# Where the last quarter of an output projection stands: between the values of the seventh and the eighth head

## What is computed

```python
z = rmsnorm(h) @ w_in                        # q latent, kv latent, rope key, and q, f, i, g of the recurrence
q = rmsnorm(cq) @ w_uq ; ckv = rmsnorm(...)  # 8 heads of 64 + 32, chunk-causal mask
o_mla = softmax(q k^T) v                     # attention over meta tokens and the blocks so far
S = diag(f_t) S + (1 - f_t) i_t^T            # gated recurrence, 4 heads of 128 x 128
o_hg = rmsnorm(S^T q_t) * silu(g)
h = h + concat(o_mla, o_hg) @ w_o            # output projection, 1024 x 1024
h = h + moe(rmsnorm(h))                      # top-1 group of 4, top-2 of its 4 experts, 16 experts of width 256
y = rmsnorm(h)
```

## Time and profile before

| what | us |
|---|---|
| median of 3 runs | 1286.23 (1285.06 to 1296.19) |
| the profiled execution's own time | 1288.34 |
| its span, first to last instruction | 1286.4 |
| input phase | 0 to 263.5 |
| preparation | 263.5 to 310.8 |
| passes 0 to 7 | 310.8 to 773.9 |
| pass 8 and the last projection | 773.9 to 850.7 |
| barrier and routing | 850.7 to 882.4 |
| experts | 882.4 to 1253.9 |
| combination and output | 1253.9 to 1286.4 |

### The profile page before, as it was taken

How to read it: one execution, slowest core, us unless ns; L and a number is a source line. 1 busy time by engine, 2 the same in 40 slices (tenths; PEclk the granted TensorE clock), 3 DMA queues, 4 the chain that set the end, 5 groups by cost and what they waited for, 6 DMA issues and landing times.

```text
span 1286.4 us, 18334 instructions
## 1 busy us (share of the span) xinstructions
PE 1104.2 (86%) x5855; PEld 888.5 (69%) x5855; DVE 734.0 (57%) x1348; ACT 519.3 (40%) x935; POOL 376.3 (29%) x378
## 2 busy tenths in 40 slices
PE   5999999969878989899899999945889899898940
PEld 4898899945466777777777786734667777677730
DVE  4320510146656656656465654447776778777866
ACT  4434122123422222322323222305777778777713
POOL 2100400001621111101010101103565666666657
PEclk9999999978989899999999998976999999999985
DMA  7340141141787666574545453805987676776567
GB/s 268 95 152 1 58 136 48 48 105 43 261 268 279 220 214 216 209 247 162 197 148 197 148 181 139 294 33 196 328 284 258 225 260 229 252 237 213 221 220 262
DMA packets 105765, 242.84 MB, mean 189 GB/s; under 512 B 15248, under 2 KB 63840, under 8 KB 95456
## 3 DMA queue, kind: packets, MB, share of 16 engines
q0 software_dynamic: 23328, 122.17, 27.1%
q1 hardware_dynamic: 81600, 117.94, 27.0%
q10 hardware_dynamic: 768, 1.84, 0.4%
HBM read 243.31 MB, written 48.94 MB: 227 GB/s over the span
## 4 chain that ended last, share of the span: by engine, by line
PE 56%; DMA 11%; DVE 10%; issue 9%; ACT 6%; POOL 4%; SPq 2%; POOLq 1%; ACTq 0%; DVEq 0%
DMA below<-in_w 8%; PE ps L1007 6%; PE ps L879 4%; PE ps L897 4%; PE ps L2103 4%; PE ps L2105 4%; PE ps L2104 4%; PE ps L966 3%; DVE low L1761 3%; PE ps L1045 3%; PE ps L1046 3%; PE ps L1049 3%; PE ps L2098 3%; PE ps L2097 3%; PE ps L2099 2%
## 5 line engine op out<-in xcount | busy, mean ns | idle before, releaser
L1761 DVE TENSOR_TENSOR low<-below,high 128x1024 fp32r<-128x1024 f32 x128 | 192.1, 1547 | 72.9 <-ACT high L1459 59.7
L1429 POOL TENSOR_TENSOR low<-below,high 128x1024 fp32r<-128x1024 f32 x64 | 146.5, 2307 | 105.9 <-ACT high L1480 105.9
L1557 PE MATMUL ps<-high 128*128 128x512 f32 x384 | 157.8, 411 | 15.3 <-DVE low L1771 10.6
L1559 PE MATMUL ps<-high,low 128*128 128x512 f32 x384 | 152.5, 397 | 0.0
L1558 PE MATMUL ps<-low,high 128*128 128x512 f32 x384 | 152.1, 396 | 0.0
L1459 ACT ACTIVATE high<-below 128x1024 fp32r<-128x1024 f32 x128 | 129.4, 1052 | 44.0 <-DMA below<-in_w 43.9
L616 ACT ACTIVATE arena<-ps 128x512 f32<-128x512 f32 (+8 forms) x100 | 51.7, 527 | 190.7 <-PE ps L879 190.2
L879 PE MATMUL ps<-arena 128*128 128x128 f32 (+4 forms) x613 | 96.7, 282 | 12.1 <-ACT arena L859 3.4
L762 POOL DMA_DIRECT2D high<-wo_dram x34 | 18.8, 552 | 295.9 <-PE ps L1049 285.1
L1956 POOL TENSOR_SCALAR arena<-arena 128x1 f32<-128x1 f32 (+5 forms) x38 | 19.1, 502 | 275.5 <-ACT arena L837 118.8
L1557 PEld LDWEIGHTS ps<-high 128*128 128x128 f32 x384 | 73.7, 192 | 35.5 <-issue 18.5
(11 more groups left out here) (240 smaller groups left out, 2251.0 us busy)
## 6 DMA issues: line engine op xcount, KB each, us to landing
below<-in_w SPq DMA_DIRECT2D x256, 256.0 KB
high<-wo_dram POOLq DMA_DIRECT2D x36, 1024.0 KB, 5.3
low<-wo_dram POOLq DMA_DIRECT2D x36, 1024.0 KB, 7.7
below<-in_w POOLq DMA_DIRECT2D x64, 512.0 KB
y_dram<-arena SPq DMA_DIRECT2D x32, 512.0 KB, 6.4
arena<-in_x_prompt SPq DMA_DIRECT2D x15, 512.0 KB
below<-in_w_in SPq DMA_DIRECT2D x14, 512.0 KB, 7.8
out<-arena SPq DMA_DIRECT2D x9, 512.0 KB, 2.6
```

The costliest lines, as they stand in the source:

```text
L1429: pool.tensor_tensor(w2_lo[s % UN][:, c], w2_in[:, c], w2_hi[s % UN][:, c].bitcast(F32), ALU.subtract).then_inc(s_w2lo, 1)
L1557: pe.matmul(out, x_hi, w_hi, start=start, stop=False)
L1559: return pe.matmul(out, x_lo, w_hi, start=False, stop=stop)
L1761: dve.tensor_tensor(chunk(w13_lo[j], c), chunk(w13_in, c), chunk(w13_hi[j], c).bitcast(F32), ALU.subtract).then_inc(s_w13lo, 1)
```

## The change

Five edits, all in the diff.

1. In passes 1 to 7 quarter 3 of the projection leaves its place behind the eighth `score` and stands between `attn` of the seventh and of the eighth head (heads 6 and 7); `sq` goes from before to behind `attn` 7; `hk` goes ahead of `hn` and `hnt`. Pass 8 keeps its order.
2. In the preparation ScalarE's queue issues the loads of `w_uk` and `w_uv`, and SyncE issues `w_uq` behind the loads of f, q, v and g instead of ahead of them.
3. The barrier after the heads' phase: GpSimd sends its increment with a write of one column in place of a drain; VectorE drains and increments, but waits for the others only inside the routing, ahead of the first write to memory that the heads' phase used.
4. PE makes four products of 128 x 512 columns that nobody reads after the routing's last products (`WARM`).
5. One column at the end of the memory is taken for the write of 3.

```diff
+WARM = 4
+    spare = Region(arena_floats - 4).take(1)
-    WO_AT = [{2: 0, 3: 1, 5: 2, 7: 3}] * (NT - 1) + [{2: 0, 3: 1, 4: 2, 5: 3}]
+    WO_AT = [{2: 0, 3: 1, 5: 2}] * (NT - 1) + [{2: 0, 3: 1, 4: 2, 5: 3}]
...
         STEPS.append(("attn", i, 6))
         if 0 < i < NT - 1:
+            STEPS.append(("wo", i - 1, WO_PARTS - 1))
+        STEPS.append(("attn", i, 7))
+        if 0 < i < NT - 1:
             STEPS.append(("sq", i - 1, 0))
-        STEPS.append(("attn", i, 7))
+        if i + 1 < NT:
+            STEPS.append(("hk", i + 1, 0))
         if 0 < i < NT - 1:
             STEPS.append(("hn", i - 1, 0))
         if i:
             STEPS.append(("hnt", i - 1, 0))
-        if i + 1 < NT:
-            STEPS.append(("hk", i + 1, 0))
         STEPS.append(("mpv", i, 0))
...
-        sp.dma_start(wuk, w_uk[0].rearrange("c h n -> c (h n)")).then_inc(s_wkv, 16)
-        sp.dma_start(wuv, w_uv[0].rearrange("c h n -> c (h n)")).then_inc(s_wkv, 16)
-        sp.dma_start(wuq, w_uq[0].rearrange("(c p) h n -> p c (h n)", p=P)).then_inc(s_wuq, 16)
         for slot in range(Z_STAGE):
             sp.wait_ge(s_stage[slot], 16 * len(range(slot, len(Z_SLOT), Z_STAGE)))
         load_fq(0)
         load_vg(0)
+        sp.dma_start(wuq, w_uq[0].rearrange("(c p) h n -> p c (h n)", p=P)).then_inc(s_wuq, 16)
...
     def attention_act(act):
+        act.dma_start(wuk, w_uk[0].rearrange("c h n -> c (h n)")).then_inc(s_wkv, 16)
+        act.dma_start(wuv, w_uv[0].rearrange("c h n -> c (h n)")).then_inc(s_wkv, 16)
...
         ins.then_inc(s_tokt, 1)
+        for n in range(WARM):
+            pe.matmul(ps[:, 5, :], tab[:, C_ID:C_ID + P], tab[:, C_ID:C_ID + 512], start=True, stop=True)
...
+        dve.wait_ge(phase_end, 8)
         dve.memset(seg.rearrange("p (e t) -> p e t", e=NE)[:, :, 1:], 1.0)
...
         attention_pool(pool, rsqrt_mean)
-        end_phase(pool, 1)
+        pool.memset(spare, 0.0).then_inc(phase_end, 1)
+        pool.wait_ge(phase_end, 8)
...
         attention_dve(dve, link)
-        end_phase(dve, 1)
+        dve.drain().then_inc(phase_end, 1)
         moe_dve(dve, link)
```

## The result

The changed kernel takes **1303.77 us** in the median of 4 runs (1302.21 to 1305.79), beside 1288.20 (1285.06 to 1296.19) for four of the kernel before: ratio **1.0105, 95% interval 1.0077 to 1.0133**, some 13.5 us slower (9.9 to 17.1); the two medians as they stand lie 15.6 apart. Its profiled execution took 1303.35 us, its span is 1301.4. So it is slower by about 1%, and 1303.77 is inside the range of 1275 to 1307. The forecast of 1296 was 8 us short of this median, and 4 short of 1286.2 x 1.0105 = 1299.7.

The account below looks back on a forecast made before the run. TensorE was taken to bound the passes, the other engines' longest chain the barrier and routing. Edits 1 to 4 summed 17.5 - 3.0 - 5.0 + 0 = +9.5 us on the 1286.2 median: about 1296, range 1275 to 1307.

Parts of the forecast that it names:

- a wait that did not happen: TensorE waiting at the next tile's first level product for `hs`: 3.3 us late in pass 3.
- the add: The add of quarter 3 at the pass end: predicted 4.1 us later in pass 3, 5.3 in pass 6.
- The wait for q: Sign: VectorE's wait for q at `hs` grows to 3 us and more in passes 2 to 4.
- The q chain: Add of quarter 3, row's store, landing, residual, f and q loads, `hs`: costs 13.5 us in passes 1 to 4.
- `hn` chain: Square, root, `hn`, meta logits: 2.5 us late in pass 3, 1.2 in pass 6; nothing extra in passes 1 to 4.
- the rival "slower": TensorE's new waits at pass ends lower its clock, 1.7 to 3.5 us per stretch, some +10: 1306; chance 0.22.
- a move of the passes' clock by more than 0.01: Sign that the forecast is wrong: the passes' granted TensorE clock, 0.95 before, changes by more than this.
- Those stay where they are: TensorE's waits in passes 0 to 7 for copies or exponentials, most of 38 us, stay unchanged; no gain taken.
- PE cannot get back more than its 3.60: Edit 2 in the preparation: TensorE's 3.60 us wait for `hs` at the first level product caps the gain; -3.0 taken.

Follow-up runs that it names:

- one chain shortened: Changed kernel with f and q loaded before the row's store and landing, ratio 1.0102; or, separately, with `hn` moved behind `mpv`, ratio 1.0116.
- both chains shortened: Changed kernel with f and q loaded before the row's store and `hn` moved behind `mpv`, together: 1294.48 us, ratio 1.0027.
- the filler: Changed kernel with q loaded early and four unread 128x512 products per pass ahead of TensorE's wait for the meta transpose: 1307.36 us, ratio 1.0129.
- one unread product: Changed kernel with a single unread 128x512 product per pass ahead of TensorE's wait for the meta transpose, passes 1 to 7: 1304.95 us, ratio 1.0118.

## Why the prediction was right, and where it was not

| step | predicted us | measured us |
|---|---|---|
| edit 1 | +17.5 | +24.7 (0.0192, from both sides; alone 19 to 30) |
| edit 2 | -3.0, at most -3.6 | -5.8 at its stage; -3.2 (-6.7 to +0.1) in the whole run alone |
| edit 3 | -5.0 | -5.1 at its stage; -3.6 (-7.5 to +0.1) alone |
| edit 4 | 0 | not told from 0 within some 5 us (1.0105 and 1.0104) |
| sum | +9.5 | +13.5 (9.9 to 17.1) |

The total missed by 4 us, the term of edit 1 by 7, and 17.5 is below the 19 to 30 of edit 1 alone. The other edits gave 7 (the two alone) to 11 us (edit 1 undone) instead of 8, which the intervals do not tell apart. That the term of edit 1 came as near as it did is luck: most of it was counted for a wait that did not happen, and what did happen had no term.

**Right:** edit 1 is the loss, edits 2 and 3 gains, and the chains' lengths. Counted from the start of the pass, the add came 4.0 us later in pass 3 and 5.3 in pass 6 (4.1 and 5.3 predicted), from there to `hs` it stayed 15 to 16 us in passes 2 to 6, and to the meta logits 4.9. The wait for q grew; 3 us and more only in passes 4 and 6 (2.5, 0.6, 3.0, 1.5 and 3.9 us in passes 2 to 6).

**The q chain did not carry the time.** The sum took 13.5 us in passes 1 to 4 from it and said that the `hn` chain "runs beside the longer q chain and costs nothing more". It was the other way round: TensorE meets the `hn` chain first, is held there (10.8 us against 2.9), and reaches the first level product so much later that q is hardly missed. The prediction decided which of two parallel chains is "the longer" by the time at which VectorE is ready; TensorE's own queue decides which it meets, and how late it is by then. The runs with one chain shortened (1.0102, 1.0116) and with both (1.0027) show that the two cover each other. With the `hn` chain gone TensorE did stand 10.2 us at the first level product, 4.0 of them in passes where that edit had lengthened the q chain. So the 13.5 us stood in the sum for a chain that by itself gave nothing back.

**The clock was left out of the sum.** It was the rival "slower", with chance 0.22: waits of TensorE take the clock along. That rival's mechanism happened on top of the forecast. 11.1 of the passes' 24.0 us are the same 2225 rows at a lower clock, that is 1.6 us a pass, just under the 1.7 to 3.5 that the rival gave for a stretch. That the waits take the clock along is shown where they were filled (busy without the filler as before the change, above); that each slower product of the changed kernel goes back to one of these waits is not. (Pass 8's eight logit products, 7.07 us there, took 5.38 in the changed kernel, whose pass 8 was 0.8 us shorter.)

The page TensorE: Matmul & The Clock Gate of the Trainium skill (Why this matters for your kernels) says that idle gaps of TensorE between bursts bring the low clock back, and speaks of long ones. The trace agrees in direction and goes further: no gap of TensorE in these seven passes is longer than 2.1 us (1.7 before), and the clock fell to its lower level in six of them (in all seven before); the weighing behind the wait took 2.08 us, 1.13 with the wait filled. The prediction named a move of the passes' clock by more than 0.01 as a sign that it is wrong. It moved by 0.02 (0.95 to 0.93 in passes 0 to 7), so by its own sign the forecast missed a part, though the time is in its range.

**The cover that quarter 3 gave was costed at nothing.** "Those stay where they are" of TensorE's other waits failed by 3.7 us: the level 7 product (1.3 to 3.6) and the transposes (2.2 to 3.6) lost the twelve products that ran while VectorE and ScalarE worked for them; with edit 1 undone both are back at 1.3 and 2.2. That quarter 3 now covers a copy between heads 6 and 7 bought little: TensorE's waits for VectorE's copies before it weighs fell from 2.9 to 2.3 us over the seven passes.

**Edit 2** was mis-sized for the same reason as edit 1. "PE cannot get back more than its 3.60" holds for the wait and not for the clock: from 263 us to the first `meta` TensorE works 33.4 us at 0.88 in place of 35.8 at 0.83. And q landed 5.1 us sooner rather than 2.7: of this 1.7 us is the earlier issue, 3.3 the shorter landing. The rule of the page DMA: Bandwidth & Descriptors of the Trainium skill (Issuing engines are not separate DMA queues), that another issuing engine saves only the time of issuing, was not separated from the move of `w_uq`, since both were made at once; nothing here speaks against it.

**The experts' phase**, +3.2 us to the end, is not the change's as far as these runs tell. From first to last slot the kernel with the same code there took 337.2 us (edit 1 undone); without the warm-up it was 343.4 (edit 1 undone) and 340.5 (edit 1 in place); the changed kernel took 342.8, the kernel before 339.7.

What stays open: the 15 us of edit 1 that remain with both chains shortened, of which only the 3.7 us of waits above have a place; and why one unread product did not do for the clock what four did.

## What to carry to other kernels

When work is moved off the place where it filled TensorE's queue, follow every chain that ends in TensorE behind it, in the order in which TensorE meets them; the first holds it, and hides the next. Shortening one of two such chains shows nothing, so test both together before a chain is cleared, and look whether the edit that shortens one lengthens the other, as `hn` behind `mpv` did through SyncE's queue. And put the clock into the sum: compare busy time of the same rows and the granted clock in both traces, since here each microsecond of added standing came with 0.7 to 1.4 us of slower products (12.9 and 11.1 in the changed kernel, 16.0 and 10.9 without the warm-up, 12.3 and 17.6 with edit 1 alone).

## What had not been expected

- An f32 product of 128 x 512 columns costs some 0.9 us at full clock (four of them, 8 rows, in 3.65 us), so four as filler are longer than the holes of 1.0 to 2.1 us.
- The warm-up puts the first gathered row's transposes at full clock, 1.07 us against 1.94, and the second slot starts 8.1 us behind the first in place of 11.8; but TensorE then stands 3.93 us for VectorE's split and the third slot comes 13.6 us later in place of 8.4. Without the warm-up the same two steps are 10.9 and 10.7 us. What was won was waited away within one slot.
- The same experts' phase, in the same code, took 342.8 us in one profiled execution and 337.2 in another.
